# RMSNorm weights folded into the projection weights on GpSimd, rstd applied by the turning matmul

## The chip, the cores and the metric

The kernel runs on one core of a Trainium2 chip. The metric is the device time of one execution in microseconds. A core has TensorE (PE in the profile, its weight loads PEld), VectorE (DVE), ScalarE (ACT), GpSimd (POOL) and SyncE (SP), which here issues most of the DMAs.

## What is computed

One layer of a streaming encoder: an RMSNorm, one wide input projection, two groups of heads that share it (windowed attention and gated linear attention), gates, an output projection and the residual. The change lies in the first lines:

```python
def rmsnorm(x, g):
    xf = x.astype(jnp.float32)
    y = xf * lax.rsqrt(jnp.mean(xf * xf, axis=-1, keepdims=True) + EPS)
    return (y * g.astype(jnp.float32)).astype(x.dtype)
...
    xn = rmsnorm(x, norm_g)
    h = xn @ w_in
```

`x` has 1024 prompt rows and 128 sample rows of 2048 elements, `w_in` is 2048 x 5648, `norm_g` has 2048 elements. All data are float32.

## The kernel before

**Tiling.** The 1152 tokens are nine tiles of 128 (`t` = 0 to 8). A projection is computed transposed, output columns on the partitions: an *item* `j` is one block of 128 columns of `w_in` against all tokens, in three groups of 384 tokens (`n` = 0 to 2), each over 16 blocks of 128 rows (`k`). To keep float32 accuracy with one-pass products, both operands are held as a high part (type fp32r) and the rest, and every product is three matmuls: `w_lo` with `x_hi`, `w_hi` with `x_lo`, `w_hi` with `x_hi` (lines 1830 to 1832). `x_hi` and `x_lo` stay in SBUF for the whole kernel.

**The lead.** Tile by tile: SyncE loads `x` (`load_x`, line 341) into one of three buffers. ScalarE squares and sums it (`sum_of_squares`, line 1661), VectorE makes the variance (`variance`, 1950), GpSimd makes rstd with a power (1616), VectorE multiplies the tile in place by rstd and by `g_row`, the norm weights copied to all partitions by a 1 MB DMA (line 1957). TensorE turns the tile into four PSUM banks with 16 transposes against the identity (`turn_x`, 1807), ScalarE copies each bank to `x_hi` (`high_halves`, 1651) and VectorE subtracts to get `x_lo` (`low_halves`, 1944). The order on each engine is written by hand. On ScalarE, tile `t`'s four copies come before the sum of squares of tile `t+2`. On VectorE the order for tile `t` is: the product (1957), the first two subtractions of tile `t-1`, the variance of tile `t+1`, the last two subtractions of tile `t-1`. A bank of tile `t+1` can be turned only when the same bank of tile `t` has been subtracted (semaphore `s_xlo`). From `t` = 3 on, TensorE does a third of a group of item 0 behind each turning (5 or 6 blocks `k`, 15 or 18 matmuls; `THIRDS`).

**The weights.** `load_w` (line 382) fetches an item's 128 columns in four quarters (`s_w[0..3]`) into the one buffer `raw`; a quarter is fetched when GpSimd has finished with the same quarter of the item before. `split` (542) does for each quarter: `w_hi` = the raw weights in type fp32r, written by adding zero (548), and `w_lo` = raw minus `w_hi` (552). `w_hi` and `w_lo` are single buffers as well: a quarter may be overwritten when TensorE is through with it in the last group of the item before (`s_wfree`, the waits on PE at line 548). TensorE's next item waits for each quarter (`s_wready`). `split_v` does the same for the 272 value and low-rank columns in pieces of 1088 elements. After the lead, items 0 to 9 are queries and keys, then come the items beside which the attention, the cached attention and the linear attention are computed, and last the output projection, which has weights of its own.

## Time and profile before

| | us |
|---|---|
| median of 3 runs | 1795.19 |
| lowest and highest | 1794.94 and 1797.36 |
| the profiled execution | 1795.29 |
| its span | 1793.5 |
| TensorE busy | 1765.4 |
| VectorE busy | 781.0 |
| GpSimd busy | 529.4 |
| ScalarE busy | 505.8 |

The span is from the first to the last instruction of the core; 1.8 us of the profiled execution lie around it. TensorE's busy time includes the modelled ends of its matmuls. What matters of the busy times is the place of the gaps, which the views by stretch and the timelines show.

### The profile page before, as it was taken

The page shows a single profiled execution, that of the slowest core. Times are in us where ns is not written, and L with a number is a line of the kernel's source. Part 1 is how long each engine was busy: PE and PEld are TensorE (multiplying, and loading weights), DVE is VectorE, ACT ScalarE, POOL GpSimd, SP SyncE. Part 2 cuts the span into 40 slices and gives each one's busy share as a digit, 9 for nine tenths or more (in the row PEclk, how much of TensorE's full clock was granted, in tenths as well). Part 3 has the DMA queues.
Part 4 walks back from the last instruction along what each step waited for, and adds up shares of the span by engine and source line. Part 5 has one row for each costly group of instructions (what it writes and reads, how often), then busy time and mean ns, then how long its engine had stood idle before and what let it go on. Part 6 is the DMA issues. An engine that isn't in the chain of part 4 may idle for free.

```text
span 1793.5 us, 30031 instructions
## 1 busy us (share of the span) xinstructions
PE 1765.4 (98%) x10741; PEld 1638.5 (91%) x10741; DVE 781.0 (44%) x1641; ACT 505.8 (28%) x1155; POOL 529.4 (30%) x486
## 2 busy tenths in 40 slices
PE   5999999999999999999999999999999999999998
PEld 5999999989999999999999999999999888878887
DVE  7754540554545421111556666652222543454333
ACT  6311110134333310000344444330011443333332
POOL 4256420322232242332655555542332000000000
PEclk9999999999999999999999999999999999999999
DMA  7432211343444332212333423344534665765654
GB/s 252 142 92 69 85 48 51 91 112 95 112 111 123 93 101 66 77 57 73 102 96 95 129 87 96 91 125 147 165 103 159 200 230 164 220 207 164 198 165 133
DMA packets 246126, 220.78 MB, mean 123 GB/s; under 512 B 26018, under 2 KB 210676, under 8 KB 244596
## 3 DMA queue, kind: packets, MB, share of 16 engines
q1 hardware_dynamic: 171828, 176.68, 31.6%
q10 hardware_dynamic: 74232, 43.23, 8.9%
q8 instruction: 40, 0.66, 0.2%
q14 instruction: 26, 0.21, 0.0%
HBM read 169.71 MB, written 52.24 MB: 124 GB/s over the span
## 4 chain that ended last, share of the span: by engine, by line
PE 95%; DVE 1%; DMA 1%; ACT 1%; issue 0%; POOL 0%; SPq 0%; ACTq 0%; DVEq 0%; POOLq 0%
PE p L1830 20%; PE p L1832 19%; PE p L1831 19%; PE p L1921 7%; PE p L1923 7%; PE p L1925 7%; PE p L896 2%; PE p L592 1%; PE p L1865 1%; PE p L1864 1%; PE p L1866 1%; PE p L620 1%; PE p L1807 1%; PE p L604 1%; PE p L908 1%; PE p L914 1%
## 5 line engine op out<-in xcount | busy, mean ns | idle before, releaser
L1830 PE MATMUL p<-x_hi,w_lo 128*128 128x384 f32 x2016 | 698.0, 346 | 0.0
L1832 PE MATMUL p<-x_hi,w_hi 128*128 128x384 f32 x2016 | 675.5, 335 | 0.0
L1831 PE MATMUL p<-x_lo,w_hi 128*128 128x384 f32 x2016 | 674.5, 335 | 0.0
L1830 PEld LDWEIGHTS p<-x_hi,w_lo 128*128 128x128 f32 x2016 | 379.0, 188 | 15.6 <-issue 13.5
L548 POOL TENSOR_TENSOR w_hi<-raw,small 128x512 fp32r<-128x512 f32 x164 | 173.5, 1058 | 726.6 <-PE p L1832 710.4
L1831 PEld LDWEIGHTS p<-x_lo,w_hi 128*128 128x128 f32 x2016 | 379.4, 188 | 0.2
L1832 PEld LDWEIGHTS p<-x_hi,w_hi 128*128 128x128 f32 x2016 | 378.6, 188 | 0.0
L2110 DVE TENSOR_TENSOR w_lo<-raw,w_hi 128x512 fp32r<-128x512 f32 x192 | 132.1, 691 | 203.4 <-ACT w_hi L1778 203.4
L552 POOL TENSOR_TENSOR w_lo<-raw,w_hi 128x512 fp32r<-128x512 f32 x164 | 216.2, 1318 | 12.8
L1778 ACT ACTIVATE w_hi<-raw 128x512 fp32r<-128x512 f32 x192 | 121.0, 633 | 238.1 <-PE p L1925 209.7
L1921 PE MATMUL p<-w_hi,x_lo 128*128 128x512 f32 x576 | 162.1, 390 | 1.1 <-DVE w_lo L2110 1.0
L1923 PE MATMUL p<-w_lo,x_hi 128*128 128x512 f32 x576 | 161.7, 389 | 0.0
L1925 PE MATMUL p<-w_hi,x_hi 128*128 128x512 f32 x576 | 161.7, 389 | 0.0
L1921 PEld LDWEIGHTS p<-w_hi,x_lo 128*128 128x128 f32 x576 | 107.8, 188 | 24.6 <-DVE w_lo L2110 2.4
L1923 PEld LDWEIGHTS p<-w_lo,x_hi 128*128 128x128 f32 x576 | 108.1, 188 | 22.5
L1925 PEld LDWEIGHTS p<-w_hi,x_hi 128*128 128x128 f32 x576 | 108.1, 188 | 22.5
L2004 DVE RECIPROCAL xn<-xn 128x384 f32<-128x384 f32 x30 | 76.6, 2553 | 18.9 <-ACT xn L1679 18.9
L2021 DVE TENSOR_TENSOR xn<-xn 128x384 f32<-128x384 f32 (+1 forms) x48 | 41.5, 880 | 98.5 <-ACT xn L1684 98.5
L1987 DVE COPY xn<-p 128x384 f32<-128x384 f32 x36 | 20.1, 558 | 132.7 <-PE p L1832 117.5
L1684 ACT ACTIVATE xn<-p 128x384 f32<-128x384 f32 x48 | 22.6, 491 | 174.9 <-PE p L1832 174.8
L740 DVE CUSTOM_DVE_ANT_0 work<-p,work,sink_row 128x192 f32<-128x192 f32 x128 | 45.8, 415 | 30.1 <-PE p L592 27.9
L679 ACT ACTIVATE work<-p 128x384 f32<-128x384 f32 x64 | 31.5, 493 | 91.0 <-PE p L605 90.9
(185 smaller groups left out, 1771.8 us busy)
## 6 DMA issues: line engine op xcount, KB each, us to landing
raw<-in_w_out SPq DMA_DIRECT2D x192, 256.0 KB, 3.4
raw<-in_w_in SPq DMA_DIRECT2D x164, 256.0 KB, 4.3
h_t<-xn SPq DMA_DIRECT2D x126, 192.0 KB, 1.9
work<-h_t SPq DMA_DIRECT2D x24, 384.0 KB, 6.0
out<-work SPq DMA_DIRECT2D x36, 256.0 KB, 4.4
work<-h_t ACTq DMA_DIRECT2D x16, 512.0 KB, 4.6
work<-h_t ACTq DMA_DIRECT2D x32, 256.0 KB, 3.9
work<-in_x_prompt SPq DMA_DIRECT2D x32, 256.0 KB, 5.1
```

The source lines that it names most:

```text
L548: pool.tensor_tensor(w_hi[:, k:k + 4, 0:n], w_raw(j, k, n), zeros[:, :].unsqueeze(1) .to_broadcast([P, 4, n]), ALU.add).then_inc(s_whi, 1)
L552: pool.tensor_tensor(w_lo[:, k:k + 4, 0:n], w_raw(j, k, n), w_hi[:, k:k + 4, 0:n].bitcast(F32), ALU.subtract).then_inc(s_wready, 1)
L740: dve.tensor_tensor_reduce(out=a_p[i][:, r, :], in0=bank_s[r % 2][:, (r // 2) * SPAN:(r // 2) * SPAN + SPAN], in1=a_mask[:, 2 * (r % 2), : ...
L1778: act.activation(o_hi[k % 4], o_raw[k % 4], ACT.Copy).then_inc(t_whi, 1)
L1830: pe.matmul(out, w_lo[:, k, :], x_hi[:, k, tok], start=(k == 0), stop=False)
L1831: pe.matmul(out, w_hi[:, k, :], x_lo[:, k, tok], start=False, stop=False)
L1832: mm = pe.matmul(out, w_hi[:, k, :], x_hi[:, k, tok], start=False, stop=(k == KT - 1))
L1921: pe.matmul(out[t], x_lo[:, k, tok[t]], o_hi[k % 4], start=(k == 0), stop=False)
L1923: pe.matmul(out[t], x_hi[:, k, tok[t]], o_lo[k % 4], start=False, stop=False)
L1925: mm = pe.matmul(out[t], x_hi[:, k, tok[t]], o_hi[k % 4], start=False, stop=(k == KT - 1))
L2004: dve.reciprocal(stage[n], tmp_b).then_inc(s_nchain, 1)
L2110: dve.tensor_tensor(o_lo[k % 4], o_raw[k % 4], o_hi[k % 4].bitcast(F32), ALU.subtract)\
```

## The change

The product of VectorE on the token tile is gone. In its place:

- `norm_g` is loaded as 16 rows of 128 (`g_rows`), turned by one small matmul into PSUM and copied by VectorE to `g_col`, one column for each block `k`. The 1 MB copy to all partitions is gone. The constants with the identity are loaded second instead of fourth.
- GpSimd multiplies the raw weights in place by `g_col` before it splits them: one more instruction for each quarter. In the lead (item 0) it stands directly ahead of that quarter's split; in all other items the four multiplications stand ahead of the four splits, so the first split is behind a wait on all four quarters. `split_v` gets one more instruction of 1088 elements a piece.
- VectorE multiplies the 128 x 128 identity by rstd (`scale[t % 2]`), and TensorE turns the unscaled tile with an ordinary float32 matmul against that diagonal matrix in place of a transpose against the identity.
- There are four `x` buffers in place of three, and `load_x(3)` needs no wait. The load of item 1's weights waits for the turning of tile 5 in place of tile 8.

```diff
             load_x(0)
-            sp.dma_start(g_row, norm_g[0:1, :].to_broadcast([P, D_MODEL])).then_inc(s_norm, 16)
+            sp.dma_start(consts_sb[:, :], consts[:, 0:C_MASK0]).then_inc(s_ident, 16)
+            sp.dma_start(g_rows, norm_g.rearrange("a (k p) -> (a k) p", p=P)).then_inc(s_ident, 16)
             load_x(1)
-            sp.dma_start(consts_sb[:, :], consts[:, 0:C_MASK0]).then_inc(s_ident, 16)
             load_x(2)
...
             for k in ks:
                 pool.wait_ge(s_w[k // 4], 16 * j + 16)
+                pool.tensor_tensor(w_raw(j, k, n), w_raw(j, k, n), g_col[:, k:k + 4].unsqueeze(2)
+                                   .to_broadcast([P, 4, n]), ALU.mult).then_inc(s_wg, 1)
+            for k in ks:
+                pool.wait_ge(s_wg, 4 * j + (k // 4 + 1))
                 pool.wait_ge(s_wfree, 4 * j + (k // 4 + 1))
...
+            pe.transpose(ss_bank[:, 0:KT], g_rows, ident[0:KT, 0:KT]).then_inc(s_ident, 1)
...
-                        mm = pe.transpose(xt_bank[b][:, k * P:k * P + P], x_buf[t % 3][:, c:c + P], ident)
+                        mm = pe.matmul(xt_bank[b][:, k * P:k * P + P], x_buf[t % 4][:, c:c + P], scale[t % 2],
+                                       start=True, stop=True)
...
-                dve.scalar_tensor_tensor(out=x_buf[t % 3], in0=x_buf[t % 3], scalar=rstd[:, 0:1],
-                                         in1=g_row, op0=ALU.mult, op1=ALU.mult).then_inc(s_xn, 1)
+                dve.tensor_scalar(scale[t % 2], ident, rstd[:, 0:1], None, ALU.mult).then_inc(s_xn, 1)
```

Three places show how the instructions stand. On GpSimd between items 1 and 2, before (`CAST` converts the mask tables, lines 548 and 552 split a quarter of item 2's weights; of the four pairs two are shown):

```order
L1623 CAST tables_sb<-work 128x512 [waits s_tload]
L1623 CAST tables_sb<-work 128x512 x4
L548 TENSOR_TENSOR w_hi<-raw,small 128x512 [waits s_wfree,s_w0]
L552 TENSOR_TENSOR w_lo<-raw,w_hi 128x512 [waits s_whi]
L548 TENSOR_TENSOR w_hi<-raw,small 128x512 [waits s_wfree,s_w1]
```

The same place in the changed kernel, where line 549 is the multiplication and lines 554 and 558 are the split:

```order
L1634 CAST tables_sb<-work 128x512 [waits s_tload]
L1634 CAST tables_sb<-work 128x512 x4
L549 TENSOR_TENSOR raw<-raw,g_col 128x512 [waits s_w0]
L549 TENSOR_TENSOR raw<-raw,g_col 128x512 [waits s_w1]
L549 TENSOR_TENSOR raw<-raw,g_col 128x512 [waits s_w2]
L549 TENSOR_TENSOR raw<-raw,g_col 128x512 [waits s_w3]
L554 TENSOR_TENSOR w_hi<-raw,small 128x512 [waits s_wfree,s_wg]
```

Four multiplications and the waits for the last three quarters now stand ahead of the item's first split. On VectorE in the lead, tile 2, before (`p_3` to `p_6` are the four banks, line 1957 is the product on the tile):

```order
L1950 TENSOR_SCALAR small<-small 128x1
L1944 TENSOR_TENSOR x_lo<-p_5,x_hi 128x4x128
L1944 TENSOR_TENSOR x_lo<-p_6,x_hi 128x4x128
L1957 SCALAR_TENSOR_TENSOR xn<-xn,small,work 128x2048
L1944 TENSOR_TENSOR x_lo<-p_3,x_hi 128x4x128
```

And in the changed kernel (line 1963 is the variance, 1957 the subtraction, 1971 the scaling of the identity):

```order
L1963 TENSOR_SCALAR small<-small 128x1
L1957 TENSOR_TENSOR x_lo<-p_5,x_hi 128x4x128
L1957 TENSOR_TENSOR x_lo<-p_6,x_hi 128x4x128
L1971 TENSOR_SCALAR work<-consts_sb,small 128x128
L1957 TENSOR_TENSOR x_lo<-p_3,x_hi 128x4x128
```

The order is the same; the instruction of 2048 elements has become one of 128, and the variance still stands between the two pairs of subtractions.

## Rows read from the trace of the kernel before

**Rows 1.** the page of the kernel before, span and busy times

```profile
span 1793.5 us, 30031 instructions
...
PE 1765.4 (98%) x10741; PEld 1638.5 (91%) x10741; DVE 781.0 (44%) x1641; ACT 505.8 (28%) x1155; POOL 529.4 (30%) x486
```

**Rows 2.** stretch: busy PE, PEld, DVE, ACT, POOL; PEclk, DMA share, GB/s

```profile
0.00:31.05 31.05, 12.25 (x64) 10.58 (x65) 19.29 (x22) 19.34 (x26) 16.62 (x19) 0.92 0.77 275
31.05:55.57 24.52, 24.51 (x164) 23.39 (x163) 23.49 (x30) 18.20 (x29) 4.94 (x5) 0.97 0.47 153
```

**Rows 3.** timeline of the lead: start us, duration us, engine, line, operation, wait before

```profile
8.69 2.35 DVE L1957 SCALAR_TENSOR_TENSOR work<-work,small 128x2048 f32<-128x2048 f32 x1 [0.84 <-POOL small L1616]
...
11.14 3.67 PE L1807 MATMUL p<-consts_sb,work 128*128 128x128 f32 x16 [11.14 <-DMA consts_sb<-in_consts]
...
14.85 0.60 ACT L1651 ACTIVATE x_hi<-p 128x512 fp32r<-128x512 f32 x1 [0.26 <-PE p L1807]
15.35 1.91 ACT L1661 ACTIVATE work<-xn 128x2048 f32<-128x2048 f32 x1
```

**Rows 4.** the same timeline, token tile 3

```profile
28.69 0.15 DVE L1950 TENSOR_SCALAR small<-small 128x1 f32<-128x1 f32 x1 [0.50 <-ACT work L1661]
28.76 1.28 DVE L1944 TENSOR_TENSOR x_lo<-p,x_hi 128x512 fp32r<-128x512 f32 x2
...
29.50 1.97 PE L1807 MATMUL p<-consts_sb,work 128*128 128x128 f32 x8 [0.59 <-DVE x_lo L1944]
...
31.50 0.60 ACT L1651 ACTIVATE x_hi<-p 128x512 fp32r<-128x512 f32 x1 [0.26 <-PE p L1807]
32.00 1.91 ACT L1661 ACTIVATE work<-xn 128x2048 f32<-128x2048 f32 x1
```

**Rows 5.** timeline of TensorE, token tiles 4 and 8

```profile
31.12 0.67 PE L1830 MATMUL p<-x_hi,w_lo 128*128 128x384 f32 x1
...
35.05 1.91 PE L1807 MATMUL p<-consts_sb,raw 128*128 128x128 f32 x16
36.71 0.42 PE L1830 MATMUL p<-x_hi,w_lo 128*128 128x384 f32 x1
...
53.79 2.02 PE L1807 MATMUL p<-consts_sb,xn 128*128 128x128 f32 x16
55.57 0.42 PE L1830 MATMUL p<-x_hi,w_lo 128*128 128x384 f32 x1
```

**Rows 6.** the same timeline, fp32 products elsewhere in the kernel

```profile
892.58 0.59 PE L907 MATMUL p<-work 128*128 128x256 f32 x2
893.01 0.59 PE L908 MATMUL p<-work 128*128 128x256 f32 x2
...
380.71 1.09 PE L620 MATMUL p<-work 128*64 128x128 f32 x16
```

**Rows 7.** timeline of GpSimd and TensorE around item 2

```profile
89.85 1.04 POOL L548 TENSOR_TENSOR w_hi<-raw,small 128x512 fp32r<-128x512 f32 x1 [16.00 <-DMA raw<-in_w_in]
90.97 1.29 POOL L552 TENSOR_TENSOR w_lo<-raw,w_hi 128x512 fp32r<-128x512 f32 x1
92.22 1.03 POOL L548 TENSOR_TENSOR w_hi<-raw,small 128x512 fp32r<-128x512 f32 x1
...
93.28 0.33 PE L1830 MATMUL p<-x_hi,w_lo 128*128 128x384 f32 x1
```

**Rows 8.** timeline of DVE, GpSimd, TensorE and the sync queue, two attention items

```profile
389.60 2.56 DVE L758 TENSOR_SCALAR work<-work,small 128x192 f32<-128x192 f32 x4
390.73 0.44 PE L604 MATMUL p<-consts_sb,work 128*128 128x128 f32 x2 [1.79 <-DVE work L758]
398.16 2.34 SPq L382 DMA_DIRECT2D raw<-in_w_in  x4
403.22 1.01 DVE L758 TENSOR_SCALAR work<-work,small 128x192 f32<-128x192 f32 x4
404.56 0.38 PE L604 MATMUL p<-consts_sb,work 128*128 128x128 f32 x2
```

More of the change, by code:

```diff
@@ L114, in project @@
         small = sb("small", [P, 96])
+        g_col = sb("g_col", [P, KT])
         mhalf, zeros = small[:, 92:93], small[:, 93:94]
@@ L118, in project @@
         seq_col = consts_sb[:, C_SEQ:C_SEQ + DEC_BATCH // 2]
-        x_buf = [work[:, 0:D_MODEL], raw[:, :], xn[:, :]]
-        g_row = work[:, D_MODEL:2 * D_MODEL]
+        x_buf = [work[:, 0:D_MODEL], raw[:, :], xn[:, :], work[:, D_MODEL:2 * D_MODEL]]
+        g_rows = work[0:KT, 4 * D_MODEL:4 * D_MODEL + P]
+        scale = [work[:, 4 * D_MODEL + P * i:4 * D_MODEL + P * i + P] for i in range(1, 3)]
         squares = work[:, 2 * D_MODEL:3 * D_MODEL]
@@ L139, in project @@
         ub = banks[3:8]
-        s_norm = sem("s_norm")
         s_ident = sem("s_ident")
         s_const = sem("s_const")
-        s_x = [sem(f"s_x{i}") for i in range(3)]
+        s_x = [sem(f"s_x{i}") for i in range(4)]
         s_w = [sem(f"s_w{i}") for i in range(4)]
@@ L154, in project @@
         s_whi = sem("s_whi")
+        s_wg = sem("s_wg")
         s_wready = sem("s_wready")
@@ L169, in project @@
         s_sig = sem("s_sig")
-        s_zero = sem("s_zero")
+        s_set = sem("s_set")
         s_zst = sem("s_zst")
@@ L352, in _ @@
                 sp.dma_start(w_raw(0, 4 * q, P), w_v[:, 4 * q:4 * q + 4, Q0:Q0 + P]).then_inc(s_w[q], 16)
+            load_x(3)
             for half in range(2):
@@ L356, in _ @@
                 sp.dma_start(gq_col[rows, 1:2], kg.rearrange("a d -> d a")).then_inc(s_const, 16)
-            for t in range(3, NT):
+            for t in range(4, NT):
                 load_x(t)
@@ L378, in load_w @@
                     if type(j) is int and j == 1:
-                        sp.wait_ge(s_xt, 4 * NTP + 4)
+                        sp.wait_ge(s_xt, 4 * 5 + 8)
                     else:
@@ L483, in _ @@
             sp.dma_start(work[:, 2 * D_MODEL:2 * D_MODEL + M_ALL], tables).then_inc(s_tload, 16)
-            sp.wait_ge(s_zero, 1)
+            sp.wait_ge(s_set, 2)
             for r in range(K0 // P, V0 // P):
@@ L559, in split_v @@
             pool.wait_ge(v_w[q], 32)
+            pool.tensor_tensor(v_raw[:, ks, :], v_raw[:, ks, :], g_col[:, ks].unsqueeze(2).to_broadcast([P, 4, NV]),
+                               ALU.mult).then_inc(v_whi, 1)
+            pool.wait_ge(v_whi, 2 * q + 1)
             pool.tensor_tensor(v_hi[:, ks, :], v_raw[:, ks, :], zeros[:, :].unsqueeze(1).to_broadcast([P, 4, NV]),
                                ALU.add).then_inc(v_whi, 1)
-            pool.wait_ge(v_whi, q + 1)
+            pool.wait_ge(v_whi, 2 * q + 2)
             pool.tensor_tensor(v_lo[:, ks, :], v_raw[:, ks, :], v_hi[:, ks, :].bitcast(F32),
@@ L1616, in _ @@
                 pool.tensor_tensor(rstd, var, mhalf[:, 0:1], ALU.pow).then_inc(s_rstd, 1)
+                if t == 1:
+                    pool.wait_ge(s_ident, 34)
                 if 1 <= t < 5:
@@ L1655, in sum_of_squares @@
             def sum_of_squares(t):
-                act.wait_ge(s_x[t % 3], 16 * (t // 3) + 16)
+                act.wait_ge(s_x[t % 4], 16 * (t // 4) + 16)
                 if t >= 1:
@@ L1660, in sum_of_squares @@
                     act.wait_ge(s_var, t - 1)
-                act.activation(squares, x_buf[t % 3], ACT.Square, accum_out=ss[:, t % 2:t % 2 + 1])\
+                act.activation(squares, x_buf[t % 4], ACT.Square, accum_out=ss[:, t % 2:t % 2 + 1])\
                    .then_inc(s_ss, 1)
@@ L1798, in _ @@
         def _(pe):
-            pe.wait_ge(s_ident, 16)
+            pe.wait_ge(s_ident, 32)
+            pe.transpose(ss_bank[:, 0:KT], g_rows, ident[0:KT, 0:KT]).then_inc(s_ident, 1)
             def turn_x(t):
@@ L1876, in _ @@
             pe.wait_ge(s_xlo, 4 * NT + 4)
-            pe.wait_ge(s_ones, 1)
+            pe.wait_ge(s_set, 1)
             group(0, NG - 1, stages={(NG - 1) * KT + 2: lambda: sum_squares(0, 0),
@@ L1953, in _ @@
             variance(0)
[L1954 removed]
+            dve.wait_ge(s_ident, 33)
+            dve.tensor_copy(g_col[:, :], ss_bank[:, 0:KT]).then_inc(s_ident, 1)
             for t in range(NT):
                 dve.wait_ge(s_rstd, t + 1)
[L1957 to L1958 removed]
+                dve.tensor_scalar(scale[t % 2], ident, rstd[:, 0:1], None, ALU.mult).then_inc(s_xn, 1)
                 if t >= 1:
@@ L1973, in _ @@
             dve.wait_ge(s_xt, 4 * NT + 4)
-            dve.memset(xn[:, 5 * TN:5 * TN + PAD], 0.0).then_inc(s_zero, 1)
+            dve.memset(xn[:, 5 * TN:5 * TN + PAD], 0.0).then_inc(s_set, 1)
             dve.memset(lr[:, :], 1.0).then_inc(sl_ini, 1)
```

11 lines of the change are left out of this document (4 added, 7 removed).

## The prediction

> **What bounds the kernel now.** I read the page first: TensorE is busy for 1765.4 us, 98% of the span [rows 1]. So the change can gain only where TensorE stands still, and anything that it adds to TensorE, or to a wait of TensorE, is paid in full. The table by stretch says where that is: of the 28.1 us without TensorE work, 18.8 lie ahead of 31.05, where it is busy for 12.25 us, and from 31.05 to 55.57 it has no gap [rows 2]. The timeline of the lead then shows what paces the nine token tiles, and the timeline of GpSimd shows how much room its work on the weights has. All the time that the change can win lies ahead of 31 us; after that TensorE only waits if somebody makes it.
>
> **The lead, tile 0.** VectorE's product takes 2.35 us from 8.69, and the first transpose starts at 11.14 [rows 3]. The scaling of a 128 x 128 identity replaces it. Its nearest row is the same kind of instruction on 128x192, four of them in 1.01 us [rows 8], so I take 0.3 us, and TensorE can start at 9.0. The constants, now second in the queue behind one tile, can be there by then: before, they came behind three 1 MB loads and were the releaser at 11.14. But the first matmuls run at the lower clock of 1.2 GHz: 16 transposes take 3.67 us [rows 3], and the first tile needs twice as many instructions now (next part). [...] Before, the turning ended at 14.81. So tile 0's last copy on ScalarE, at 14.85 before, comes between 0 and 1.1 us later than it did; I take 0.3, and with it tile 2's sum of squares (15.35 before) starts at about 15.6.
>
> **The lead, tiles 1 to 3.** Four steps follow one another from there, and the change leaves all of them: ScalarE's sum of squares, the variance, the last two subtractions of the tile before (they stand behind that variance on VectorE), the turning of banks 3 and 4, ScalarE's last copy, and again the sum of squares. In the rows of tile 3 the ring goes from the variance at 28.69 through the subtraction (28.76), the transposes (29.50) and the last copy (31.50) to the next sum at 32.00 and its end 1.91 us later, at 33.9 and a little: 5.3 us from variance to variance [rows 4]. VectorE's product is not in it. Those eight transposes ran at 1.2 GHz in 1.97 us; sixteen instructions at 2.4 GHz take about the same, so the ring stays at 5.3 us a tile if the clock is high, and becomes 7.1 if it is low. Two rings after tile 2's sum (it ends at 17.6) bring tile 4's sum to its end at 28.3 and the turning of tile 3 to its end at 30.8; before, the first matmul on weights stood at 31.12 [rows 5]. That wins 0.3 us. The group behind it ran its first matmuls at 1.2 GHz and took 3.93 us to 35.05 [rows 5], where 18 matmuls at the pace of the next stretch, 221 recorded in 37.71 us or 0.17 each [rows 2], take 3.1; TensorE will be busier ahead of it, so I count those 0.8 us as won too. Lead: -1.1 us, between -2.5 and +5 (clock low for three tiles).
>
> **Turning, tiles 4 to 8.** Here TensorE has no gap to hide in. An ordinary float32 product is two instructions in this trace where a transpose is one: the products of 256 columns at lines 907 and 908 are recorded as two each, and a pair starts every 0.43 us [rows 6], which is 0.84 ns a column and instruction. For 128 columns that is 0.107 us an instruction, and 32 instructions make 3.4 us a tile. The five turnings took from 35.05 to 36.71 (1.66 us), 2.06, 2.03, 1.67 and 1.78 (53.79 to 55.57), together 9.2 us [rows 5]. The new ones take 5 x 3.41 = 17.05. **Cost: +7.9 us.** The lower bound is a product that goes as fast as line 620, 16 instructions in 1.09 us or 64 ns each [rows 6]; those write 64 partitions and can go side by side, which ours can't. The token tiles come in time, with a fourth buffer and 1 MB less ahead of them, and the other engines keep up: a tile then lasts 6.0 us or more on TensorE, and ScalarE and VectorE need 5.3.
>
> The Trainium skill, page "TensorE: Matmul & The Clock Gate", section "Terms", says that the transpose mode is four times faster for FP32. The rows say twice: 0.104 us a transpose at the full clock and 0.213 a product. By the page a product would cost 0.42 us and a turning 6.7 us; that is a rival below.
>
> **The weights on GpSimd.** The new instruction has the shape of line 548, 1.04 us for 128x512 [rows 7]. It comes 164 times, 171 us on an engine that is idle for 70% of the time; its splits waited 710.4 us for TensorE to free `w_hi`, 17 us for each of 41 items [rows 1], against 4.2 us of multiplications, which fit in there once the quarters have landed. Where that wait is short, beside the linear attention, the attention's own matmuls stretch the group during which the quarters come free, so that none is wanted at once. One item has no such wait. Item 2's weights are late: GpSimd waited for the DMA, not for TensorE, until 89.85 [rows 7]. It then splits a quarter every 2.4 us (89.85 to 92.26), and TensorE starts the item at 93.28 without a gap. The first quarter was ready at 92.26, 1.0 us early; the fourth, by that pace, at 99.5, when TensorE, at 0.52 us a block `k` and 0.35 us for a sum of squares in between, wants it at 99.9. Now the first split starts four multiplications later: 4 x 1.04 = 4.1 us, less 1.0 of room, and TensorE stands for 3.1 us; the second and third quarters, each 0.3 us slower than TensorE's 2.08, add 0.6, less 0.1 of rounding. **Cost: +3.6 us**, bounds 3.0 and 5.0 (if the multiplication goes like line 552, 1.29 us). That load does not move against TensorE: it is issued behind the store of item 0's last group, which TensorE's matmuls pace. The value weights' four extra instructions, 2.1 us each by their width, go into waits as well.
>
> **GpSimd against VectorE.** A term without a row of its own. While GpSimd's splits ran beside them, four VectorE instructions on 128x192 took 2.56 us in place of 1.01, and TensorE stood for 1.79 us at line 604 [rows 8]. In the next item the load is issued at 398.16 and lands some 4 us later, at 402.2, so the four multiplications will run from 402.2 to 406.5, right over the four instructions at 403.22, which TensorE wants at 404.56 [rows 8]. Held twice, the second of them ends near 404.9: 0.4 us late. Seven such items: +2.8 us. Beside the linear attention no row tells me VectorE's slack; I take nothing there and leave it to the bound. Together **+3.0 us**, bounds 0 and 12.6 (1.8 us in each of seven items).
>
> The Trainium skill, page "SBUF — State Buffer", section "Terms", says the same more strongly: of GpSimd and VectorE the loser blocks fully for the other's instruction. By that four multiplications could hold VectorE for 4.2 us an item. The row shows 1.55 us of holding for two instructions, so the rows' bound is the one that I use.
>
> **The sum.** Lead -1.1, turning +7.9, item 2 +3.6, contention +3.0: +13.4 us on the profiled execution's 1795.29, which is 0.1 over the median. 1808.7.
>
> **The rivals.**
> 1. *The product is as cheap as the transpose.* At line 620's 64 ns a turning takes 2.05 us: turnings +1.0, the lead 1.4 us shorter still, so -1.5 altogether, item 2 +3.6: 1797.4, not slower than the bound. For it: that row. Against: its operands are half as wide, and every full-width row has the slower pace.
> 2. *GpSimd holds VectorE and through it TensorE much longer,* 1.8 us in each attention item and as much in some of the linear ones: 1795.3 + 10.4 + 12.6 = 1818, up to 1830. For it: the row of 1.79 us. Against: TensorE stood there once, with eight such items.
> 3. *The product costs four times a transpose:* 5 x 6.7 - 9.2 = +24, the lead +5: 1831. Against: lines 907 and 908.
> 4. *Faster:* the ring in the lead breaks in a way that I don't see, and turnings hide: at best ScalarE's own work paces it (20 us of it from 5.66), TensorE starts its weights at 25.6, and with 64 ns a product that is -6: 1789 to 1791. It needs three of my terms to be wrong.
>
> **Chances.** Forecast 0.67 (1802 to 1814), rival 1 0.08, rival 2 0.15, rival 3 0.03, rival 4 0.07. A measurement tells 0.2%, 3.6 us, from no change. Faster by more: 0.07. Within it: 0.08. Slower by more: 0.85. The range takes in rival 1 and the nearer half of rival 2: 1797 to 1816.
>
> **What would show it.** The first matmul on weights at 30 to 31 us, not at 25. Two instructions for each product at the turning line, 288 in all, and 3.4 us a tile. The start of item 1's first group some 7 us later than before. In item 2 a wait of TensorE of 3 to 4 us on GpSimd's `w_lo`, the only one in the kernel. At line 604, or what it becomes, waits on VectorE in most attention items, of under 1 us. From there to the end no difference. I'm wrong if the turning takes about 2 us a tile, if TensorE doesn't wait in item 2 (the weights landed earlier against it), or if the waits in the attention exceed 1 us an item.

## The result and the profile after

The changed kernel takes 1833.5 us (median of 4 runs, 1832.2 to 1836.4), the kernel before beside it 1795.7: a ratio of 1.0214 (95% interval 1.0202 to 1.0226). It is 37.8 us slower, where 13.4 were forecast with a range up to 1816. The direction was right and the time lies outside the range.

The page of the changed kernel, its span and the busy times, and three groups of instructions (line, engine, operation, out<-in, shape, count; busy us, mean ns; idle time ahead and what ended it):

```profile
span 1830.4 us, 30633 instructions
...
PE 1788.3 (98%) x10886; PEld 1657.4 (91%) x10886; DVE 817.9 (45%) x1642; ACT 505.5 (28%) x1155; POOL 708.5 (39%) x658
...
L554 POOL TENSOR_TENSOR w_hi<-raw,small 128x512 fp32r<-128x512 f32 x164 | 175.1, 1068 | 358.5 <-PE p L1845 358.3
L549 POOL TENSOR_TENSOR raw<-raw,g_col 128x512 f32<-128x512 f32 x164 | 173.9, 1087 | 217.9 <-DMA raw<-in_w_in 217.6
```

On the page before, GpSimd's first half of a split had waited 710.4 us for TensorE, the room of 17 us an item in which the prediction placed the multiplications:

```profile
L548 POOL TENSOR_TENSOR w_hi<-raw,small 128x512 fp32r<-128x512 f32 x164 | 173.5, 1058 | 726.6 <-PE p L1832 710.4
```

They did fit: 173.9 us of multiplications at 1.09 us each, GpSimd at 39% where it was at 30% [rows 1]. But TensorE's busy time rose by 22.9 us, and its span by 36.9. The waits of TensorE in the changed kernel (us in total, times, longest) name what else happened:

```profile
PE p L613 <- DVE work L767: 11.8, 8, 1.9
PE p L1811 <- DMA work<-in_norm_g: 6.2, 1, 6.2
PE p L905 <- DVE far_q L1140: 5.2, 8, 1.1
PE p L1819 <- DVE x_lo L1957: 4.7, 3, 1.6
PE p L1843 <- POOL w_lo L558: 2.5, 1, 2.5
```

and of these the kernel before had the one behind VectorE's division, once, and the one of the turning:

```profile
PE p L604 <- DVE work L758: 1.8, 1, 1.8
PE p L1807 <- DVE x_lo L1944: 7.7, 5, 3.3
```

(The second wait, for the norm weights, stands at the start, where the kernel before waited 11.1 us for the constants.) So one of the eight waits at line 613 was there before; seven are new. Lines have moved: 758 is 767 now (VectorE's division in the attention), 604 is 613 (TensorE's transposes of the divided probabilities), 1131 is 1140 (VectorE's products in the linear attention), 896 is 905 (the TensorE products that need them), 1807 is 1819 (turning), 1830 is 1843, 548 and 552 are 554 and 558, 1944 is 1957.

**Where the time went, by starts.** Cutting each trace at the first or last start of a line on TensorE gives lengths in us. "Squares" is the first start of the sums of squares (line 1841), "values" the first start of the third matmul of the token values (1866), "scores" line 592 (first and last start), "linear" line 851 (first and last start), "output" the first start of line 1921, all numbered as before. The table holds all kernels of this study. Each row is the profiled execution of its kernel, which need not be the median one (e4's took 5.2 us more than its median, e5's 3.6 less).

| kernel | start to squares | squares to values | values to scores | attention: first to last scores | to linear | linear: first to last | to output |
|---|---|---|---|---|---|---|---|
| before | 59.3 | 190.2 | 110.6 | 263.1 | 241.6 | 307.0 | 222.8 |
| changed | 67.2 | 194.5 | 110.7 | 277.8 | 241.7 | 315.4 | 224.3 |
| e1, no multiplications | 66.5 | 190.2 | 110.6 | 263.3 | 241.8 | 307.6 | 222.8 |
| e2, none in attention | 65.9 | 195.0 | 110.6 | 263.2 | 241.5 | 315.2 | 224.6 |
| e3, none in linear | 65.9 | 195.2 | 110.6 | 276.6 | 241.6 | 308.0 | 225.2 |
| e4, transposes | 56.2 | 195.0 | 110.7 | 279.3 | 242.0 | 315.0 | 225.2 |
| e5, behind the chain | 65.8 | 195.1 | 110.7 | 263.1 | 241.6 | 307.6 | 224.3 |
| e7, quarter by quarter | 67.2 | 202.2 | 111.9 | 263.2 | 246.1 | 316.6 | 233.6 |
| e8, narrow | 66.4 | 198.5 | 110.7 | 263.2 | 241.6 | 308.6 | 222.9 |
| e9, two turnings | 54.5 | 196.6 | 110.7 | 277.9 | 241.6 | 314.8 | 224.3 |
| e10, item 2 | 67.2 | 192.6 | 110.6 | 274.9 | 241.6 | 315.2 | 224.7 |
| e11, row by product | 60.1 | 190.3 | 110.6 | 263.0 | 242.3 | 308.0 | 222.8 |
| e12, all three treated | 55.0 | 192.8 | 110.7 | 263.1 | 241.9 | 307.5 | 224.4 |
| e13, and the load ahead | 55.9 | 190.2 | 110.7 | 263.1 | 241.6 | 307.4 | 222.9 |

The changed kernel loses 7.9 us up to the squares (lead and turning), 4.3 in the next stretch (item 2), 14.7 in the attention, 8.4 in the linear attention and 1.5 behind it. The last three, 24.6 us, were forecast at 3.0.

**The turning** went as forecast. TensorE's timeline of the changed kernel, tiles 0 to 4 and the first weights matmul:

```profile
8.90 6.69 PE L1819 MATMUL p<-work 128*128 128x128 f32 x32 [2.42 <-DVE work L1971]
15.43 1.95 PE L1819 MATMUL p<-work,raw 128*128 128x128 f32 x16
18.96 2.05 PE L1819 MATMUL p<-work,raw 128*128 128x128 f32 x16 [1.58 <-DVE x_lo L1957]
20.84 1.95 PE L1819 MATMUL p<-work,xn 128*128 128x128 f32 x16
...
31.59 0.42 PE L1843 MATMUL p<-x_hi,w_lo 128*128 128x384 f32 x1
...
34.80 3.73 PE L1819 MATMUL p<-work 128*128 128x128 f32 x32
```

A tile is 32 instructions and takes 3.5 us at the full pace; tile 0 ran at half of it throughout (0.209 us an instruction, 6.7 us), the pace of 1.2 GHz; the ring is 5.4 us a tile (15.43, 20.84).

**Item 2** is GpSimd's timeline, and TensorE's wait at its end:

```profile
97.40 4.03 POOL L549 TENSOR_TENSOR raw<-raw,g_col 128x512 f32<-128x512 f32 x4 [15.66 <-DMA raw<-in_w_in]
101.39 1.04 POOL L554 TENSOR_TENSOR w_hi<-raw,small 128x512 fp32r<-128x512 f32 x1
102.51 1.26 POOL L558 TENSOR_TENSOR w_lo<-raw,w_hi 128x512 fp32r<-128x512 f32 x1
...
103.82 0.69 PE L1843 MATMUL p<-x_hi,w_lo 128*128 128x384 f32 x1 [2.46 <-POOL w_lo L558]
```

Four multiplications stand ahead of the first split of weights that came late, as the prediction had it for the kernel before's late load [rows 7]. The wait is 2.5 us, the stretch 4.3 us longer. The other 1.8 us lie in the matmuls behind the wait: they start 0.32 us apart, where the usual distance is 0.17, and the granted clock is 0.50 (columns as in [rows 2]):

```profile
103.80:106.90 3.10, 3.08 (x10) 3.08 (x11) 0.38 (x1) 0.00 (x0) 3.02 (x3) 0.50 0.00 0
```

**The attention** is where the surprise lies. One item, GpSimd, VectorE and TensorE:

```profile
416.10 4.09 POOL L549 TENSOR_TENSOR raw<-raw,g_col 128x512 f32<-128x512 f32 x4 [3.54 <-DMA raw<-in_w_in]
...
416.09 0.17 DVE L754 TENSOR_SCALAR small<-small 128x4 f32<-128x4 f32 x1
416.30 0.89 DVE L756 TENSOR_TENSOR small<-sink_row,small 128x4 f32<-128x4 f32 x1
...
417.50 3.03 DVE L767 TENSOR_SCALAR work<-work,small 128x192 f32<-128x192 f32 x4
...
419.43 0.43 PE L613 MATMUL p<-consts_sb,work 128*128 128x128 f32 x2 [1.11 <-DVE work L767]
```

The same chain of VectorE in the kernel before, in one of the items of [rows 8]:

```profile
402.50 0.17 DVE L745 TENSOR_SCALAR small<-small 128x4 f32<-128x4 f32 x1
402.70 0.16 DVE L747 TENSOR_TENSOR small<-sink_row,small 128x4 f32<-128x4 f32 x1
```

From the chain's first row to the end of the second division it was 1.3 us before (402.50 to 403.77) and is 3.2 now (416.09 to 419.29). A division took up to 1.09 us beside multiplications of 1.05 us, and an operation on four elements per partition took 0.89 in place of 0.16. Not everything was held: the reciprocal of the same chain, at 417.29, ran in 0.18 us in the middle of a multiplication.

**The linear attention** shows it with other instructions. After and then before:

```profile
989.48 4.66 POOL L549 TENSOR_TENSOR raw<-raw,g_col 128x512 f32<-128x512 f32 x4
...
990.85 1.08 DVE L1137 TENSOR_TENSOR work<-work 128x384 f32<-128x384 f32 x1 [0.30 <-ACT far_q L990]
991.86 3.62 DVE L1140 TENSOR_TENSOR far_q<-work,far_q 128x384 f32<-128x384 f32 x3
...
995.61 1.56 PE L905 MATMUL p<-far_q,work 128*128 128x192 f32 x8 [0.60 <-DVE far_q L1140]
```

```profile
960.79 0.56 DVE L1128 TENSOR_TENSOR work<-work 128x384 f32<-128x384 f32 x1 [0.31 <-ACT far_q L981]
961.27 1.09 DVE L1131 TENSOR_TENSOR far_q<-work,far_q 128x384 f32<-128x384 f32 x3
```

1.6 us of VectorE's work became 4.6. These are the products of the tile's last level. Before, nothing of GpSimd's ran beside them: the weights had landed, but the split waited for TensorE to free `w_hi`. A multiplication works in `raw`, waits for no such thing, and starts at once.

### The profile page after: what moved, and what is told of

It reads as the page before. It is cut to its first block, busy times and chain, and to the rows that moved or that the text cites. A ratio compares the mean times of both kernels' runs of the same rounds, so it can differ in the third digit from the quotient of the medians.

```text
span 1830.4 us, 30633 instructions
## 1 busy us (share of the span) xinstructions
PE 1788.3 (98%) x10886; PEld 1657.4 (91%) x10886; DVE 817.9 (45%) x1642; ACT 505.5 (28%) x1155; POOL 708.5 (39%) x658
## 4 chain that ended last, share of the span: by engine, by line
PE 85%; DVE 4%; issue 4%; POOL 3%; ACT 2%; DMA 1%; ACTq 0%; SPq 0%; DVEq 0%; POOLq 0%
PE p L1843 17%; PE p L1845 16%; PE p L1844 16%; PE p L1934 7%; PE p L1936 7%; PE p L1938 7%; PE p L1819 2%; PE p L601 1%; POOL work L1231 1%; POOL far_q L1231 1%; DVE far_q L1140 1%; PE p L1878 1%; PE p L1877 1%; PE p L1879 1%; PE p L613 1%
## 5 line engine op out<-in xcount | busy, mean ns | idle before, releaser
L1843 PEld LDWEIGHTS p<-x_hi,w_lo 128*128 128x128 f32 x2016 | 379.5, 188 | 18.4 <-issue 13.6
L549 POOL TENSOR_TENSOR raw<-raw,g_col 128x512 f32<-128x512 f32 x164 | 173.9, 1087 | 217.9 <-DMA raw<-in_w_in 217.6
```

The lines of the kernel that those rows point to most:

```text
L549: pool.tensor_tensor(w_raw(j, k, n), w_raw(j, k, n), g_col[:, k:k + 4].unsqueeze(2) .to_broadcast([P, 4, n]), ALU.mult).then_inc(s_wg, 1)
L1843: pe.matmul(out, w_lo[:, k, :], x_hi[:, k, tok], start=(k == 0), stop=False)
```

## The experiments

The theory from here on: GpSimd's multiplications hold VectorE, instruction by instruction, while it works on the chain that TensorE waits for; this costs about 24.5 us on top of the turning and item 2. The rivals: the product turning or the shifted loads change the pace elsewhere, or GpSimd's added time as such is what costs.

### Taking the multiplications away: all, attention, linear

e1 takes the multiplications, and the waits on them, out of `split` and out of `split_v`, for all weights. e2 and e3 leave them out in `split` for items 11 to 18 and for items 27 to 34 alone, and keep the semaphore's count:

```
+                if mult:
+                    pool.tensor_tensor(w_raw(j, k, n), w_raw(j, k, n), g_col[:, k:k + 4] ..., ALU.mult).then_inc(s_wg, 1)
+                else:
+                    pool.sem_inc(s_wg, 1)
```

> The changed kernel without any of GpSimd's multiplications by the norm weights, those of the value weights included (so the weights are not scaled by them); the lead and the turning product stay. Theory A (the multiplications hold VectorE, and TensorE waits for VectorE, on top of what the lead, the turning and item 2 cost): what is left is the lead and the turning, 7.9 us by the first squares' starts, so 1795.7 + 7.9 = 1803.6 us, 1802 to 1805.5, and TensorE has no wait at line 613 above one of 2 us, none at line 905 and none on w_lo. Rival B (the product turning leaves the rest of the kernel at another pace, through clock or queues): 1815 or more. Rival C (as I forecast before: only item 2 and 3 us hang on the multiplications): 1826.

1803.8 us (ratio 1.0046, interval 1.0029 to 1.0062), where theory A had 1803.6. Every stretch but the first is within 0.6 us of its length before.

> The changed kernel, with the multiplications left out for the eight items whose weights are staged beside the eight attention tiles (items 11 to 18, so these weights are not scaled). Theory A: the waits for VectorE's division in attention and what the clock loses behind them go away, 14.8 us, and nothing else: 1833.4 - 14.8 = 1818.6, 1817.5 to 1820. Rival B (it is the later start of each item against its weight loads, or the changed turning, that shifts VectorE against TensorE): under 4 us are won, 1829 or more.

1819.2 us (1.0133), 14.3 less than the changed kernel. The attention is back at 263.2, and the rest is as in the changed kernel to within 1.3 us.

> The changed kernel, with the multiplications left out for the eight items whose weights are staged beside the eight tiles of linear attention (items 27 to 34, not scaled). Theory A: the 9.8 us that the linear attention lost come back, and nothing else: 1823.6, 1822.5 to 1825; TensorE's waits for VectorE's products in far_q are gone. Rival B: part of the loss is GpSimd's own queue (its differences for the next tile stand behind the multiplications): the same total, but the changed kernel would then show waits for GpSimd, which the trace does not; or the loss is elsewhere, then 1830 or more.

1825.4 us (1.0168), 8.1 less, a little short of theory A, which asked for at most 1825 (its 9.8 had counted in the 1.5 us behind the linear attention, which stayed). Linear is at 308.0. So the loss hangs on the multiplications, stage by stage.

### Their place and their width

e5 leaves all the work and moves its start:

```
+                if after and k == 0:
+                    pool.wait_ge(*after)
...
+                split(pool, j, after=(sa_p, 16 * (j - (J_ATT + 1)) + 8))
...
+                split(pool, j + 1, after=(sl_zz, NZ * (j - J_GLA) + NZ))
```

> The changed kernel with the same multiplications, but later: in the eight attention items the first of the four waits until VectorE has done the divisions of the tile's first two groups, in the eight linear items until VectorE has done its last products for the tile. Theory A (the loss hangs on GpSimd's multiplications running beside VectorE's instructions that TensorE waits for): nearly all that the two leaving-out runs won comes back with no work removed, 14.3 + 8.1 = 22.4 us: 1833.4 - 22.4 = 1811, 1809.5 to 1815; what stays are the turning and item 2's wait. Rival B (the loss is GpSimd's added time as such, its queue being longer): 1830 or more, or slower than the changed kernel, since the splits come later.

1812.7 us (1.0099, interval 1.0082 to 1.0116; runs from 1809.1 to 1815.0): 20.7 less with no work removed. Attention 263.1, linear 307.6. Rival B falls: GpSimd's added time as such costs nothing there. (The profiled execution, in the table, is the shortest of the four.) GpSimd now waits for VectorE instead of the other way round:

```profile
L551 POOL TENSOR_TENSOR raw<-raw,g_col 128x512 f32<-128x512 f32 x164 | 168.6, 1058 | 275.7 <-DMA raw<-in_w_in 187.0 <-DVE work L769 64.7 <-DVE far_q L1142 23.8
```

e8 leaves the place and cuts each instruction in four:

```
+                for i in range(4):
+                    one = pool.tensor_tensor(w_raw(j, k, n)[:, i, :], w_raw(j, k, n)[:, i, :],
+                                             g_col[:, k + i:k + i + 1].to_broadcast([P, n]), ALU.mult)
+                one.then_inc(s_wg, 1)
```

> The changed kernel with each multiplication of 128x512 cut into four of 128x128; same place, same elements. In the changed kernel VectorE's divisions of 0.31 us took up to 1.09 us beside multiplications of 1.05 us: one division got in between two multiplications. Theory A (VectorE is held for the length of one GpSimd instruction, and gets in where GpSimd changes instructions): with instructions of 0.3 us a division takes at most 0.35 to 0.6 us, the eight waits shrink from 1.4 us each to 0.5 or less, and 8 to 15 us are won: 1818 to 1826. Theory B (VectorE is slowed by the traffic in SBUF, whatever the length of an instruction): divisions still take about 1 us, 1832 or more.

1813.2 us (1.0098): 20.3 less, more than theory A asked for, though GpSimd spends 250.2 us on them in place of 173.9 (0.42 us each, x656). VectorE's four divisions beside sixteen narrow multiplications:

```profile
418.05 5.92 POOL L550 TENSOR_TENSOR raw<-raw,g_col 128x128 f32<-128x128 f32 x16 [3.56 <-DMA raw<-in_w_in]
...
418.81 1.61 DVE L769 TENSOR_SCALAR work<-work,small 128x192 f32<-128x192 f32 x4
```

They took 1.61 us, where it was 3.03 beside wide ones and 1.01 alone [rows 8]. Traffic in SBUF had not become less, only the instructions shorter. So these operations of VectorE are held for about the rest of the GpSimd instruction under way, and get in where GpSimd changes instructions. Item 2 pays for it (198.5 in place of 194.5).

e7 moves each multiplication to its own split, behind the wait for TensorE:

```
             for k in ks:
                 pool.wait_ge(s_w[k // 4], 16 * j + 16)
+                pool.wait_ge(s_wfree, 4 * j + (k // 4 + 1))
                 pool.tensor_tensor(w_raw(j, k, n), w_raw(j, k, n), g_col[:, k:k + 4] ..., ALU.mult).then_inc(s_wg, 1)
-            for k in ks:
```

> The changed kernel with each multiplication moved directly ahead of its own quarter's split, behind the wait for TensorE to free that quarter, in every item. Nothing is left out. Theory A: the multiplications leave the stretch in which the weights have just landed, so the eight waits at line 613 and those at line 905 as they were go away; but three instructions a quarter (3.4 us) now stand against the 2.1 us in which TensorE uses a quarter, so the last quarter of an item is ready 3.4 x 4 = 13.6 us after the first is free, where TensorE wants it 14.7 us after: no new wait for w_lo except in item 2, where it stays at 3 to 4 us. 1811 to 1818, the wider end because the splits run longer beside VectorE. Rival B (GpSimd's room is smaller than that): waits for w_lo in many items, 1825 or more.

1841.8 us (1.0253), the slowest of all. The attention is back at 263.2, so that half of theory A held; but my sum for GpSimd's room did not, and rival B has it:

```profile
PE p L1842 <- POOL w_lo L557: 15.7, 25, 1.4
PE p L934 <- DVE work L1114: 6.7, 7, 1.0
```

25 waits of at most 1.4 us for `w_lo`: by my sum 1.1 us of room (14.7 against 13.6) is too little once anything holds GpSimd. The other wait is on VectorE at another place of the linear attention; its cause is open. So the room of 17 us an item lies ahead of the first free quarter, not behind it.

### The turning and the lead

e4 puts the transposes back, e9 keeps the product for tiles 0 to 3 alone:

```
-                        mm = pe.matmul(xt_bank[b][:, k * P:k * P + P], x_buf[t % 4][:, c:c + P], scale[t % 2],
-                                       start=True, stop=True)
+                        mm = pe.transpose(xt_bank[b][:, k * P:k * P + P], x_buf[t % 4][:, c:c + P], ident)
```

> The changed kernel, with transposes on the plain identity in place of the product with the diagonal (so the tokens are not scaled by rstd); everything else, VectorE's scaling of the identity and GpSimd's multiplications, stays. Theory A: five turnings in the filled stretch cost 3.49 us each instead of 1.84, 8.2 us, and the lead's ring waits less at 16 instructions a tile: 1833.4 - 8.2 = 1825.2, with the lead 1824 to 1826. Rival B (the ring in the lead is paced by TensorE's products too): 2 to 4 us more are won, 1821 to 1823. Rival C (the turning also shifts the later items against their loads and so sets the waits in attention): the result lies outside 1821 to 1827.

1819.5 us (1.0130; 1818.3 to 1824.6), 14.0 less than the changed kernel. That is outside 1821 to 1827, so the result goes with rival C by its own words. The trace is of the longest execution (1824.6) and shows no reason for the rest. In it the squares come 11.0 us earlier: 3.3 by the lead, where tile 0 takes 3.7 us and not 6.7 and the first weights matmul stands at 28.33 (31.59), and the rest by the turnings. That is rival B. Behind them the attention is 1.5 us longer than in the changed kernel. The mean granted clock is 0.993 where the others have 0.995 to 0.997, and from 16.00 to 29.65, in the lead, it is 0.50. So the others had less time at the low clock; whether that makes all of their 4 to 6 us, or whether the waits in the attention moved too, as rival C has it, no trace shows.

> The changed kernel with the product with the diagonal for tiles 0 to 3 only, while TensorE has little else to do; tiles 4 to 8 are scaled by rstd on VectorE and turned by transposes as in the kernel before. For tiles 0 to 3 all four subtractions of the tile before now stand ahead of the variance. The multiplications stay as they are. Theory A: the filled stretch loses its 7.9 us, the ring in the lead (5.4 us a tile) falls to 4.2 to 4.6 us, so the first matmul on weights stands at 27 to 29 instead of 31.6: 1833.4 - 8 - 3 = 1822, 1819 to 1825. Rival B (VectorE's scaling of a tile, 2.2 us and more beside GpSimd's multiplications, paces tiles 4 to 8): TensorE waits there, 1826 or more.

The edit beside e4's, on VectorE:

```
+                if t < 4:
+                    dve.tensor_scalar(scale[t % 2], ident, rstd[:, 0:1], None, ALU.mult).then_inc(s_xn, 1)
+                else:
+                    dve.tensor_scalar(x_buf[t % 4], x_buf[t % 4], rstd[:, 0:1], None, ALU.mult).then_inc(s_xn, 1)
+                first = 4 if t < 4 else 2
```

1821.0 us (1.0140), 12.4 less, as in theory A. The squares start at 54.5, 4.8 us ahead of the kernel before: the product is worth having where TensorE idles, and not where it is full. How much of the 4.8 us is the earlier turning, the loads or the new order of the subtractions was not told apart; e4, with the old order and no scaling of the tile, stands at 56.2.

e11 asks whether that lead can be had in the kernel before. The norm row comes as 8 KB and is spread by TensorE:

```
+            for i, c, n in ((0, 0, 512), (0, 512, 512), (0, 1024, 128), (1, 1152, 384), (1, 1536, 512)):
+                row = g_one[i][:, c - 1152 * i:c - 1152 * i + n]
+                mm = pe.matmul(xt_bank[c // 512][:, c % 512:c % 512 + n], ones_one, row, start=True, stop=True)
```

> The kernel before, nothing of the change in it but what the lead gained: the norm weights' row comes as 8 KB on one partition and is spread over the partitions by TensorE (ones times row, five products, while it has nothing else to do) and four copies, in place of the 1 MB load ahead of tile 1; constants load ahead of tile 1; VectorE's product of tile 0 goes in four pieces, so the first transpose waits for a quarter of it. Theory A (what the lead of the changed kernel wins with transposes, first weights matmul at 28.3 instead of 31.1, comes from tile 1 landing 1.5 us earlier and tile 0 being turned 2 us earlier): first weights matmul at 28.3 to 29.3, 1795.5 - 2.3 = 1793.2, 1792.5 to 1794.2, faster than both. Rival B (it comes from VectorE's 2.35 us product being gone from each tile): no change, 1795 to 1796.

1798.9 us (1.0021, interval 1.0012 to 1.0030): slower, neither theory. Tile 1 was indeed summed 1.7 us earlier (9.10, from 10.81), but the products of 512 columns took 7.2 us, and the last of VectorE's four copies, which I had put ahead of tile 0's variance, ended at 10.5:

```profile
2.57 4.20 PE L1805 MATMUL p<-work 1*128 1x512 f32 x6 [2.57 <-DVE work L1965]
6.57 3.19 PE L1805 MATMUL p<-far_q,work 1*128 1x384 f32 x4
...
9.80 0.69 DVE L1968 COPY work<-p 128x512 f32<-128x512 f32 x1 [1.01 <-PE p L1805]
```

So tile 0 was turned at 12.24, not 11.14. I had not priced these products: two instructions each, and a product of 512 columns every 1.7 us. Which of the two theories is right stays open.

### Item 2, and the three together

e10 gives three of item 2's multiplications to VectorE, behind item 1's second group:

```
+            dve.wait_ge(s_wg, 4 * 2 + 1)
+            for c in range(4, KT, 4):
+                dve.wait_ge(s_w[c // 4], 16 * 2 + 16)
+                dve.tensor_tensor(w_raw(2, c, P), w_raw(2, c, P), g_col[:, c:c + 4] ..., ALU.mult).then_inc(s_wg, 1)
```

> The changed kernel with one item altered: item 2's multiplications of quarters 2 to 4 are done by VectorE, in its gap behind item 1's second group, at the pace of its other 128x512 subtraction (0.69 us mean), while GpSimd multiplies and splits the first quarter. Theory A (TensorE's wait for w_lo in item 2, 2.5 us recorded and 4.2 us by the starts around it, is GpSimd's four multiplications ahead of the first split of weights that land late): the wait goes, 3.5 to 4.5 us: 1829 to 1830. Rival B (the weights land so late that TensorE waits anyway): 1832 or more, with the wait now ending on the DMA.

1828.5 us (1.0191), 5.0 less. Theory A's number is nearly met, but not its reason. Item 2's stretch gives 1.9 of that (192.6), and TensorE still waits twice for `w_lo`, 1.7 us together where it was 2.5: GpSimd's second split, beside VectorE's multiplications, took 1.42 and 1.59 us where the first took 1.04 and 1.29. The rest of the 1.9 is the clock, which is not low behind these waits. The attention gives 2.9 us, and there too it is the clock: it is 1.00 throughout, where the changed kernel has two stretches at 0.50 (below). So in this experiment the multiplications' share in the stall is 0.8 us. e12 puts e5, e9 and e10 into one kernel.

> The changed kernel with its three losses treated at once: the product turning for tiles 0 to 3 only, the multiplications of the attention and linear items behind VectorE's chain, and item 2's shared with VectorE. Theory A (the three are independent and add up): 1833.4 - 12.4 (two turnings) - 20.7 (behind the chain) - 4 (item 2) = 1796.3, within 1793.5 to 1799, so level with the kernel before: what the lead wins (4.8 us, by the start of the first squares) is used up by what stays. Rival B (they share a part, since an earlier start of item 2 moves every later item against its loads): 1800 or more.

1796.0 us (1.0008, interval 0.9999 to 1.0017), level with the kernel before: the three add up as theory A had it. Against the kernel before it wins 4.3 us up to the squares and loses 2.6 in item 2 and 1.6 behind the linear attention. For both e13 has a remedy, the first of which takes out e10's share again:

```
-            sp.dma_start(win_ks[:, 0:old, :], cache_k[:, DEC_SEQ:CACHE, :]).then_inc(s_win, 16)
-            sp.dma_start(win_vs[:, 0:old, :], cache_v[:, DEC_SEQ:CACHE, :]).then_inc(s_win, 16)
...
                 load_w(q + 2, (q + 1) * P + (Q0 + P), P)
+                if q == 0:
+                    sp.dma_start(win_ks[:, 0:old, :], cache_k[:, DEC_SEQ:CACHE, :]).then_inc(s_win, 16)
+                    sp.dma_start(win_vs[:, 0:old, :], cache_v[:, DEC_SEQ:CACHE, :]).then_inc(s_win, 16)
...
+            pool.wait_ge(sl_zz, NZ * NTP + 2 + len(DEC_LEVELS))
```

> The kernel with the three losses treated, once more, with two things altered. Item 2: VectorE no longer shares the multiplications; instead the two copies of the cached keys and values (1.8 MB) are issued behind item 2's weight load, not ahead of it, so the load, 11.0 us from issue to landing in the kernel before, should take 4 to 5. Item 35: its multiplications wait for VectorE's last products of the decoding tile. Theory A (item 2 loses only because its weights land late behind those copies; 2.6 us there and 1.6 us around item 35 are what keeps the treated kernel level with the kernel before): 1796.0 - 2.6 - 1.5 = 1792, 1791 to 1793.5, no wait for w_lo, and faster than both kernels. Rival B (GpSimd's room in item 2 is short whatever the load does, or the copies then collide with the value weights' load): 1795 or more.

1791.8 us (0.9979, interval 0.9970 to 0.9988; 11 runs against 15): faster than the kernel before by 3.9 us and than the changed one by 41.7. Both remedies show in the table (190.2 and 222.9). Item 2's weights, before and in e13 (count, KB each, us from issue to landing):

```profile
raw<-in_w_in SPq DMA_DIRECT2D x4, 256.0 KB, 11.0
```

```profile
raw<-in_w_in SPq DMA_DIRECT2D x4, 256.0 KB, 3.8
```

With the load ahead GpSimd has multiplied all four quarters (77.1 to 81.3) before TensorE frees the first, at 83.6.

## Why the prediction was wrong

| term | forecast | by the traces |
|---|---|---|
| lead | -1.1 | -0.25 (first turning of tile 4 at 34.80, from 35.05) |
| turning, tiles 4 to 8 | +7.9 | +8.2 (3.49 us a tile, from 1.84) |
| item 2 | +3.6 | +4.3 |
| GpSimd against VectorE, attention | +2.8, with the rounding +3.0 | +14.7 |
| the same, linear attention and behind it | 0 | +9.9 |
| sum | +13.4 | +36.9 |

**The lead.** Its reasoning held: the ring is 5.4 us where 5.3 was said, TensorE starts at 8.90 where 9.0 was said. The clock in tile 0 was the part left between bounds, and the 0.3 us taken for it no row showed. The pace did not rise within tile 0, which took 6.7 us; ScalarE's last copy of it came 0.8 us later than before (15.63, from 14.85), and the first weights matmul at 31.59 in place of 30.8. It moves from one execution to the next: in e2, with the same lead code, tile 0 took 5.2 us, that copy came 0.6 us earlier than before (14.25), outside the bounds of 0 and 1.1, and the first weights matmul stood at 30.21. The group behind ran at the full pace and took 3.2 us (31.59 to 34.80); 3.1 was forecast from this stretch of the kernel before (columns as in [rows 2]):

```profile
55.57:93.28 37.71, 37.71 (x221) 37.71 (x219) 24.13 (x28) 9.72 (x18) 15.86 (x16) 1.00 0.45 154
```

**The turning.** Two instructions a product and 0.109 us each: right, from [rows 6]. The Trainium skill's page "TensorE: Matmul & The Clock Gate" (section "Terms") says that the transpose mode is four times as fast for FP32, from which the prediction estimated 6.7 us a tile; the trace shows 3.5, twice the 1.84 of transposes. Rival 3 is out, and so is rival 1.

**Item 2.** Right in mechanism, and nearly in size by luck: TensorE waited once, for 2.5 us, where 3.1 and 0.6 were summed, and the low clock behind the wait, which the sum had not, made up 1.8. The prediction took the late load for given. e13 shows why it was late: 1.8 MB of cache copies issued just ahead of it.

**GpSimd against VectorE is the step that failed**, by 21.6 of the 23.5 us that are missing. The mechanism was named, as a term and as rival 2, and three things in its working were wrong.

1. *What is held.* I counted the two divisions of [rows 8] and took 1.55 us for them. The four multiplications lie over the whole chain ahead of them too, and a small operation can be held as long as a large one: the one of 0.16 us took 0.89. The trace of the kernel before had shown it in the very item of [rows 8]: at 388.21, ahead of the divisions, an operation on four elements took 1.14 us beside a split. The chain ran 1.9 us longer, not 1.1. Against the 0.8 us of slack that [rows 8] give, 0.4 became 1.1 in this item and up to 1.9 in others. The number of items was right: the eighth of the waits is the one of 1.8 us that the kernel before has too. Seven new ones make 10.0 us where 2.8 were forecast, and waits over 1 us an item were the prediction's own sign of being wrong.
2. *The linear attention.* "Beside the linear attention no row tells me VectorE's slack; I take nothing there and leave it to the bound." A missing row was read as zero. The three products of VectorE at the end of each tile were as plain in the trace as the divisions, with GpSimd just done with its own part and the next weights in place; the change moved GpSimd's work onto them. That is 8.4 us, 5.8 of them in waits of TensorE and 2.6 in its busy time (at a clock of 1.00, cause open), and 1.5 in the decoding tile behind.
3. *What a wait costs besides.* In the attention TensorE stands 10.0 us longer by its waits, but the stretch is 14.7 longer. The rest is in its busy time, and the granted clock is below 1 where it was 1.00:

```profile
372.40:650.20 277.80, 265.76 (x2240) 240.22 (x2240) 154.61 (x535) 99.80 (x370) 98.19 (x88) 0.99 0.39 103
```

```profile
360.10:623.20 263.10, 261.01 (x2241) 238.13 (x2240) 133.44 (x535) 100.16 (x370) 65.64 (x57) 1.00 0.42 109
```

(Changed kernel, then before; stretch, busy PE, PEld, DVE, ACT, POOL, granted clock, DMA share, GB/s.) With the same 2240 matmuls TensorE is busy for 4.75 us more. Most of it lies in two stretches with the granted clock at 0.50, each about 1 us behind a wait of 1.9 us. This is the second (the first is at 404.04):

```profile
530.34:533.75 3.41, 3.41 (x22) 2.68 (x24) 1.15 (x4) 0.50 (x2) 0.00 (x0) 0.50 0.16 58
```

At half the pace 3.4 us of work cost 1.7 more, so the two make 3.4; the other 1.3 us no experiment explains. The length of the attention goes with their number: none in e10 (274.9), one in e3 (276.6), two in the changed kernel, e9 and e4 (277.8, 277.9, 279.3). The waits that they stand behind are not all new, nor does each wait bring one: behind its own wait of 1.8 us the kernel before has none, and the changed kernel has one behind the same wait. e2, without the multiplications there, has a clock of 1.00 and 261.05 us. VectorE's column shows the holding itself, 154.6 us for the same 535 instructions that took 133.4; e5 has 140.6.

The Trainium skill's page "SBUF — State Buffer" (section "Terms") says that of GpSimd and VectorE the loser blocks fully. It says so of one instruction, and the trace agrees for the divisions: one took 1.09 us beside a multiplication of 1.05. The reciprocals it shows unheld, 0.18 us. My step in the prediction from there to 4.2 us for four in a row does not follow: VectorE got an instruction in at each change between GpSimd's, and e8 shows that it gets in more often when these are shorter. I had set that sentence aside for the row's 1.55 us. The row was measured beside splits that VectorE met once in eight items; the multiplications met it in every item.

Rival 2 named the mechanism and the stages, 1818 to 1830 by 1.8 us in each attention item and some linear ones, and got 0.15; the measured 1833.5 lies beyond its end. "TensorE stood there once, with eight such items" was the argument against it, though the prediction had just worked out that the change would put GpSimd over that chain in every item.

## What to carry to other kernels

Room on an engine is no room in time. Before work is added to GpSimd, find which VectorE instructions it will lie over, count all of the chain up to what TensorE waits for, small ones too, and look in a trace which of them are held; price each of those at one GpSimd instruction. If the work must be added, let it wait for VectorE's chain (20.7 us here with no work removed) or cut it into short instructions (20.3 us here). A new wait of TensorE also has a price behind it where its clock falls, 1.7 us a time here. A stage with no row of the effect needs a price from its nearest row, not zero. And an operation that costs twice as much on TensorE belongs where TensorE idles; kept to the lead, with its loads and a new order of the subtractions, the edit won 4.8 us there; in the filled stretch the turnings had lost 8.2.

## What the runs showed of the hardware

- The half pace of the start does not show as a granted clock. Over tile 0's turning in the changed kernel (stretch; busy PE, PEld, DVE, ACT, POOL; granted clock, DMA share, GB/s) the column reads 1.00, while an instruction takes twice as long as in tile 4:

```profile
8.90:15.40 6.50, 6.50 (x32) 6.50 (x33) 1.73 (x4) 3.79 (x5) 3.23 (x4) 1.00 1.09 353
```

- Later falls do show. Behind the wait of 2.5 us in item 2 the column reads 0.50, with matmuls 0.32 us apart in place of 0.17. Behind waits of 1.8 and 1.9 us it fell in some places of these runs and not in others.
- Several kinds of VectorE operations with their operands in SBUF are held by a GpSimd instruction that is under way: a division (TENSOR_SCALAR) of 0.31 us became 1.09, and a TENSOR_TENSOR of 0.16 became 0.89. With GpSimd instructions of 0.42 in place of 1.05 us four divisions took 1.61 in place of 3.03 us. A RECIPROCAL in SBUF was not held (0.18 us at 417.29, inside a multiplication), and neither were VectorE instructions that read PSUM: the six masked copies of line 1162 took 1.37 us beside a multiplication, and 1.37 alone.
- A multiplication of 128x128 on GpSimd took 0.42 us and one of 128x512 1.05: by an estimate from these two about 0.2 us of each is not in the elements.
- Two DRAM to DRAM copies of 0.9 MB ahead of it made a weight load of 1 MB take 11.0 us from issue to landing, 3.8 without them.
- In e11 fp32 products over a single partition, 512 columns wide, followed one another every 1.7 us (VectorE's copies of them start at 4.68, 6.39, 8.09 and 9.80). Tile 0's turning over 128 partitions took 0.209 us an instruction of 128 columns at the start of the changed kernel, which makes the same 1.7 us for 512 columns and two instructions: one partition is no cheaper than 128.
